# A streaming encoder step on one core: who issues a table copy, where six-row groups of gathers stand, and how a block opens

## What is computed

```
z = rmsnorm(x) @ w_in                       # 5888 columns: q,k,v of mixer A; q,k,v, gate of mixer B; two branch gates
oa = windowed attention with sinks (8 heads)
ob = retention with a state carried from block to block (4 heads)
y  = norm(ob) * silu(rg)
x1 = x + (sigmoid(ga) * (oa @ wa) + sigmoid(gb) * (y @ wb)) @ wo
h2 = rmsnorm(x1)
# expert retrieval: each row picks 128 of 16384 experts
a  = gelu(sum_d(h2 * u[idx]))               # "dots", 128 rows of u per token
x2 = x1 + sum_k(gate * a * v[idx])          # "values", 128 rows of v per token
out = rmsnorm(x2)
```

## Time and profile before

| | |
|---|---|
| median of 3 runs | 4240.19 us (4240.1 to 4246.9) |
| profiled execution: time, span | 4240.92 us, 4239.1 us |
| PE busy | 3299.9 us, 78% |
| DVE busy | 2488.8 us, 59% |
| POOL busy | 1872.0 us, 44% |
| ACT busy | 1047.1 us, 25% |
| granted PE clock, mean | 0.923 of full speed |
| DMA moved | 1554.55 MB, 367 GB/s |

### The profile page before, as it was taken

The page is one execution under the profiler, slowest core; times in us unless marked ns, Lnnn a source line. Parts: engine busy times, 40 slices in busy tenths (PEclk is TensorE's granted clock), DMA queues, the critical chain, the costliest instruction groups (busy, mean ns, idle before and its releaser), DMA issues.

```text
span 4239.1 us, 31704 instructions
## 1 busy us (share of the span) xinstructions
PE 3299.9 (78%) x8957; PEld 1646.9 (39%) x8957; DVE 2488.8 (59%) x5002; ACT 1047.1 (25%) x2851; POOL 1872.0 (44%) x1668
## 2 busy tenths in 40 slices
PE   8776599999657767638877977977977977777776
PEld 5453256666334444314333333333433432222222
DVE  0122078988846666436765765665665675675444
ACT  2111011111022122102333333333233333333332
POOL 1020147776725443203454454454454455455454
PEclk9877799999868878869999999999999999999999
DMA  9898989999978886527999999999999999999998
GB/s 354 298 297 296 317 268 413 411 413 404 385 310 309 331 321 244 193 115 302 421 421 420 406 421 406 421 419 409 407 422 411 415 421 419 415 415 422 422 420 351
DMA packets 302287, 1554.55 MB, mean 367 GB/s; under 512 B 31265, under 2 KB 58913, under 8 KB 179617
## 3 DMA queue, kind: packets, MB, share of 16 engines
q0 software_dynamic: 239616, 1342.28, 79.4%
q1 hardware_dynamic: 47920, 189.40, 11.4%
q10 hardware_dynamic: 14592, 21.10, 1.3%
HBM read 1509.02 MB, written 179.04 MB: 398 GB/s over the span
## 4 chain that ended last, share of the span: by engine, by line
DMA 27%; PE 17%; issue 6%; DVE 2%; ACT 1%; POOL 1%; POOLq 0%; ACTq 0%; DVEq 0%
DMA ring<-uv_d,IXD_p 27%; PE ps L1534 14%; PE ps L1504 3%; DVE ring L1735 1%; ACT dg L1584 1%; POOL ring L1853 1%; ACT GE_p L1578 0%; DVE DOT_p L1735 0%; DVE BV_p L945 0%; DVE ACC L1716 0%; ACTq L1583 0%; PE ps L1497 0%; PE ps L1519 0%; POOLq L1849 0%; DVE X L1726 0%
## 5 line engine op out<-in xcount | busy, mean ns | idle before, releaser
L1534 PE MATMUL ps<-ring,dg 128*128 128x512 f32 x3584 | 1698.9, 611 | 454.8 <-ACT dg L1584 433.7
L1853 POOL DMA_INDIRECT ring<-uv_d,IXD_p x896 | 1122.7, 1253 | 1330.4 <-PE ps L1534 1011.1
L1735 DVE CUSTOM_DVE_ANT_0 ring<-ring,H 128x1024 f32<-128x1024 f32 x896 | 1094.2, 1223 | 879.5 <-DMA ring<-uv_d,IXD_p 863.9
L1534 PEld LDWEIGHTS ps<-ring,dg 128*128 128x128 f32 x3584 | 651.4, 192 | 1381.6 <-ACT dg L1584 713.5
L1200 PE MATMUL ps<-w,xg 128*128 128x368 f32 x1792 | 554.3, 472 | 2.0 <-ACT SC_s L902 2.0
L1578 ACT ACTIVATE GE_p<-DOT_p 128x2 f32<-128x2 f32 x448 | 91.1, 203 | 1477.5 <-DVE DOT_p L1735 1477.5
L1200 PEld LDWEIGHTS ps<-w,xg 128*128 128x128 f32 x1792 | 340.4, 190 | 215.5 <-ACT SC_s L902 2.2
L1584 ACT ACTIVATE dg<-gdi,GE_p 128x128 f32<-128x128 f32 x896 | 310.6, 393 | 51.4 <-PE ps L1534 6.1
L1572 ACT ACTIVATE gdi<-ident,GD_p 128x128 f32<-128x128 f32 x896 | 303.0, 386 | 14.6 <-issue 14.5
L145 POOL DMA_DIRECT2D uv_d<-in_peer_u x128 | 68.3, 534 | 491.5 <-DMA uv_d<-in_peer_v 258.9
L1504 PE MATMUL ps<-wq,hT_p 128*128 128x512 f32 x448 | 224.3, 605 | 39.6 <-ACT hT_p L1542 39.6
(11 more groups left out here) (370 smaller groups left out, 2941.3 us busy)
## 6 DMA issues: line engine op xcount, KB each, us to landing
uv_d<-in_peer_u POOLq DMA_DIRECT2D x128, 512.0 KB, 6.4
uv_d<-in_peer_v POOLq DMA_DIRECT2D x128, 512.0 KB, 7.8
w<-in_w_in SPq DMA_DIRECT2D x8, 2944.0 KB, 14.9
w<-in_w_in SPq DMA_DIRECT2D x16, 1472.0 KB, 9.4
z_d<-zo ACTq DMA_DIRECT2D x16, 1288.0 KB, 18.6
ring<-uv_d,IXD_p POOLq DMA_INDIRECT x896, 11.1
gates_p<-z_d SPq DMA_DIRECT2D x7, 1536.0 KB, 10.0
wq_s<-in_peer_w_q SPq DMA_DIRECT2D x8, 1024.0 KB, 13.4
```

What stands on the lines that cost most here:

```text
L1534: mm = T.matmul(bank(6 + n), dg[:, k % DR, :], ring[:, k % RS, D + n * 512:D + (n + 1) * 512], start=(k == 0), stop=(k == NK - 1))
L1735: V.tensor_tensor_reduce(out=row, in0=row, in1=H2[:], scale=1.0, scalar=0.0, op0=ALU.mult, op1=ALU.add, accum_out=DOT[:, k:k + 1]).then_in ...
L1853: g.indirect_dma_start(ring[:, n % RS, :], None, uv_d, bass.IndirectOffsetOnAxis(ap=IXD[:, n:n + 1], axis=0)).then_inc(s_ring[n % RS], 16)
```

## The change

There are four edits.

1. The last 46 parts of the table are issued by SyncE (`rest_of_table`, a semaphore of its own, s_uvs) and no longer by GpSimd. In blocks 3 to 7 it issues three parts behind the load of the keys part, two behind the gates' load, and three at the end, behind the load of x; in block 8 two and four. GpSimd's stream in the stage is then gathers alone. The last stage waits for s_uvs too.
2. A point is cut into half points: value group (even) and dot group (odd). Three stand behind the softmax, three behind the copy of line 700, and two behind the retention norm. Dot group 1 thus stands behind the merge, and value group 2 between dot groups 1 and 2.
3. A block opens with the copies of q and k from PSUM, then the gate product; the v copy, the decayed k and the gate biases of the block before come after it.
4. Semaphore increments that nobody waits for are dropped (es, sm_neg, rok, mixa, keep).

```diff
+        s_uvs = sem("uv_table_rest")
+
+        def rest_of_table(sp, lo, hi):
+
+            for part in range(lo, min(hi, NEXP // P)):
+                sp.dma_start(uv_d[part * P:(part + 1) * P, 0:D], rows(t["peer_u"], part)).then_inc(s_uvs, 16)
+                sp.dma_start(uv_d[part * P:(part + 1) * P, D:], rows(t["peer_v"], part)).then_inc(s_uvs, 16)
+
...
                 act.wait_ge(s["sm_d"], blk + 1)
-                S.activation(es[:], es[:], ACT.Exp).then_inc(s["es"], 1)
+                S.activation(es[:], es[:], ACT.Exp)
...
                 step.settle()
-                v.sem_inc(s["rok"], 1)
...
                 V.tensor_tensor(z(RG, D), z(RG, D), yn[:].rearrange("p h n -> p (h n)"), ALU.mult).then_inc(s["ysil"], 1)
+
+            def dve_biases(v, blk):
+                v.wait_ge(s["z2"], 16 * blk + 16)
                 V.tensor_tensor(z(GA, 2 * D), z(GA, 2 * D), bg[:], ALU.add).then_inc(s["ga"], 1)
...
         def dve_block(v, blk, half, merge):
             step = Steps(v, s_vstep, STEPS_E if blk == 1 else STEPS_B + (blk - 2) * DVE_B)
+            v.wait_ge(s["t1"], blk + 1)
+            V.tensor_copy(qbT[:].rearrange("p h n -> p (h n)"), bank(1))
+            if blk <= 2:
+                v.wait_ge(s_tab, 32 * blk)
+            V.tensor_tensor(qdT[:].rearrange("p h n -> p (h n)"), bank(1), into[:].rearrange("p h n -> p (h n)"), ALU.mult)
+            V.tensor_copy(kaT[:, 1], ps[:, 3, 0:P]).then_inc(s["qkv"], 1)
+            if merge:
+                dve_gate(v, blk - 1)
+            wait_mixers(v, blk, half)
+            step.did(V.tensor_copy(va[:, 1], z(VA, P, half)))
+            for h in range(HB):
+                q = V.tensor_scalar(kdec[:, h, :], z(KB + h * DK, DK, half), outd[:, h:h + 1], None, ALU.mult)
+            q.then_inc(s["kdec"], 1)
             if merge:
                 if blk == 3:
                     v.wait_ge(s_bw, 16 * 8)
-                dve_gate(v, blk - 1)
-            wait_mixers(v, blk, half)
-            if blk <= 2:
-                v.wait_ge(s_tab, 32 * blk)
-            for h in range(HB):
-                q = V.tensor_scalar(kdec[:, h, :], z(KB + h * DK, DK, half), outd[:, h:h + 1], None, ALU.mult)
-            q.then_inc(s["kdec"], 1)
-            step.did(V.tensor_copy(va[:, 1], z(VA, P, half)))
-            v.wait_ge(s["t1"], blk + 1)
-            V.tensor_tensor(qdT[:].rearrange("p h n -> p (h n)"), bank(1), into[:].rearrange("p h n -> p (h n)"), ALU.mult)
-            V.tensor_copy(qbT[:].rearrange("p h n -> p (h n)"), bank(1))
-            V.tensor_copy(kaT[:, 1], ps[:, 3, 0:P]).then_inc(s["qkv"], 1)
+                dve_biases(v, blk - 1)
...
             dve_probs(v, blk, 2 * P)
-            dve_point(v, blk, 0)
-            dve_point(v, blk, 1)
+            for half_point in range(3):
+                dve_point(v, blk, half_point)
             if merge:
                 dve_merge(v, blk - 1)
             v.wait_ge(s["pt"], blk + 1)
             V.tensor_copy(PT[:, 4:8].rearrange("p h c n -> p (h c n)"), bank(2, 2)).then_inc(s["ptc"], 1)
-            dve_point(v, blk, 2)
+            for half_point in range(3, 6):
+                dve_point(v, blk, half_point)
             v.wait_ge(s["oat"], blk + 1)
             V.tensor_copy(oaT[:].rearrange("p j n -> p (j n)"), bank(0)).then_inc(s["oatc"], 1)
             V.tensor_copy(kaT[:, 0], kaT[:, 1])
-            V.tensor_copy(va[:, 0], va[:, 1]).then_inc(s["keep"], 1)
+            V.tensor_copy(va[:, 0], va[:, 1])
             dve_retention_norm(v, blk, 2, step)
-            dve_point(v, blk, 3)
+            for half_point in range(6, 8):
+                dve_point(v, blk, half_point)
             if merge:
                 dve_residual(v, blk - 1)
...
             def dve_point(v, blk, j):
-                grp = PTS * (blk - 2) + j
-                if blk > 2:
+                grp = PTS * (blk - 2) + j // 2
+                if j % 2:
+                    dve_expert_dots(v, grp)
+                elif blk > 2:
                     dve_expert_values(v, grp - PTS)
-                dve_expert_dots(v, grp)
...
                             load_keys_part(sp, blk + 1)
+                        part = TABLE_S + 8 * (blk - 3)
+                        if 2 < blk < NB - 1:
+                            rest_of_table(sp, part, part + 3)
+                            part += 3
                         if blk > 2:
                             sp.wait_ge(s["mixt"], blk)
                             load_gates(sp, blk)
+                            rest_of_table(sp, part, part + 2)
                             sp.wait_ge(s["x1"], blk)
                             sp.dma_start(rows(x1_d, blk - 1), X[:]).then_inc(s["x1st"], 16)
                             sp.wait_ge(s["h2"], blk)
                             sp.dma_start(rows(h2_d, blk - 1), HO[:]).then_inc(s["h2st"], 16)
                             sp.wait_ge(s["x1st"], 16 * blk)
                             load_rows(sp, blk)
+                            rest_of_table(sp, part + 2, part + 5 if blk < NB - 1 else NEXP // P)
...
                             pool_dots(g, grp)
-                            if blk > 2:
-                                part = TABLE_S + 2 * (grp - PTS)
-                                pool_table(g, part, min(part + 2, NEXP // P))
...
                     for i in range(2):
-                        g.wait_ge(s_uv[i], 32 * (NEXP // P // 2))
+                        g.wait_ge(s_uv[i], 32 * (TABLE_S // 2))
                         g.sem_inc(d["pool"], 1)
+                    g.wait_ge(s_uvs, 32 * (NEXP // P - TABLE_S))
+                    g.sem_inc(d["pool"], 1)
```

More of the change, by code:

```diff
@@ L228, in _ @@
                             mm.then_inc(s_mm, 1)
-        names = ("z1 z1b zq z2 xld t1 qkv scores sm_s sm_m sm_mx sm_neg sm_d es exp den rden prob pt ptc oat "
-                 "oatc st atm ro rok kvp stn stats var rs rstd yn silu ysil yt ytc ga gates ya mixa "
-                 "mixb mix mixt mixtc wo x1 ssq2 ms2 sq2 r2 h2 x1st h2st keep kdec").split()
+        names = ("z1 z1b zq z2 xld t1 qkv scores sm_s sm_m sm_mx sm_d exp den rden prob pt ptc oat "
+                 "oatc st atm ro kvp stn stats var rs rstd yn silu ysil yt ytc ga gates ya "
+                 "mixb mix mixt mixtc wo x1 ssq2 ms2 sq2 r2 h2 x1st h2st kdec").split()
         s = {n: sem("b_" + n) for n in names}
@@ L384, in dve_softmax @@
                 v.wait_ge(s["sm_mx"], blk + 1)
-                V.tensor_scalar(ngm[:], mx[:], -1.0, None, ALU.mult).then_inc(s["sm_neg"], 1)
+                V.tensor_scalar(ngm[:], mx[:], -1.0, None, ALU.mult)
                 V.tensor_tensor(es[:], sinks, mx[:], ALU.subtract).then_inc(s["sm_d"], 1)
@@ L426, in dve_merge @@
                 v.wait_ge(s["ya"], blk + 1)
-                V.tensor_tensor(z(GA, D), z(GA, D), bank(4, 2), ALU.mult).then_inc(s["mixa"], 1)
+                V.tensor_tensor(z(GA, D), z(GA, D), bank(4, 2), ALU.mult)
                 V.tensor_tensor(z(GB, D), z(GB, D), bank(6, 2), ALU.mult).then_inc(s["mixb"], 1)
@@ L593, in _ @@
                     dve_gate(v, 0)
+                    dve_biases(v, 0)
                     for h in range(HB):
@@ L831, in _ @@
                     V.memset(va[:, 0], 0.0)
-                    V.memset(alibi_c[:], NEG).then_inc(s["keep"], 1)
+                    V.memset(alibi_c[:], NEG)
                     V.memset(st[:], 0.0).then_inc(s["stn"], 1)
@@ L836, in _ @@
                     dve_gate(v, 1)
+                    dve_biases(v, 1)
                     dve_merge(v, 1)
@@ L1442, in _ @@
                     dve_gate(v, NB - 1)
+                    dve_biases(v, NB - 1)
                     for grp in range(LAST, TAIL - 1):
```

## The result

The changed kernel takes **4215.71 us** (median of 4 runs, 4213.54 to 4219.38), the kernel before 4242.14 (4 runs, 4240.1 to 4246.9): ratio 0.9942, 95% interval 0.9927 to 0.9956. The profiled execution took 4217.13 us (span 4215.3), 23.8 less than that of before. So it is faster, inside the range of 4183 to 4228, but the gain is 24 to 26 us where 42 were forecast.

What follows compares the result with a forecast made beforehand. No engine is full in mixer blocks 2 to 8; DVE's waits for gathers and PE's opening waits bound them. Gains of 15.2 (opening), 21.5 (copies and half points) and 5.4 (block 8) sum to 42.1, giving 4199 us, range 4183 to 4228.

Steps and rivals of the forecast that it cites:

- The bound: Whole kernel: the DMA-full last stage stays at 2313 us, so only blocks 2 to 8 of the mixer can gain.
- The opening, 15.2 us: Block openings: q and k copies fit under the silu wait, removing PE's 2.54 us wait before the scores, six times.
- The copies: Blocks 3 to 7: six of eight table parts move to where GpSimd can't put them, filling an empty DMA stretch.
- just fit: Block's end: six parts with stores and loads end about 32 us behind the dots, next value gather asked at 33.
- The half points, 21.5 us with the copies: Blocks 3 to 7: waits for gathers fall from 13.1 to 8.8 us a block, 4.3 each, 21.5 in all.
- The walk of block 7: Block 7, points replayed in the new order from time 0: the dots end at 48.7 us instead of 52.9.
- I take 3.7 (the landing then is 6.3): Block 7, second dot group: assumed wait of 3.7 us, between 1.5 and 6.5, with gates and two parts sharing the engines.
- the 9.3 of my upper bound: Second dot group: the middle landing of value gathers, 9.3 us, taken to give a wait of 6.5 us.
- what I had added to values 1 for the end of the parts: Block 7, second value group: 1.0 us added for the end of the six parts, moving its end from 15.5 to 16.5.
- PE's floor of 44.5: Block 8: PE's 44.5 us, above DVE's 44.0, sets its stretch instead of 49.9, a gain of 5.4 us.
- The signs: Profile checks: PE's scores wait gone, gated-transposes wait unchanged, openings 77 us apart, waits placed, pause's DMA busy, last stage 2313 us.
- One load, waits only move: Rival, 15%: gathers and copies are one load, landings stay near 9.3 us, only the opening gains, 4226 us.

Runs made afterwards that it cites:

- e1: Kernel before with only the new opening (q and k copies ahead of the gate product, biases and decayed k behind it): 4220.90 us, ratio 0.9954.
- e2: Kernel before with only the table copies moved to SyncE in sets of 3, 2 and 3, whole points, old opening: 4221.67 us, ratio 0.9959.
- f2: Changed kernel without the two parts behind the gates' load; four parts in the tail, twelve issued by GpSimd in the last stage: 4220.73 us, ratio 0.9872.
- e4: Changed kernel with sets of table copies 4, 0 and 4 instead of 3, 2 and 3: 4210.71 us, ratio 0.9934.

## Why the prediction was right and wrong

**The bound.** Right: nothing outside blocks 3 to 8 moved by more than 1.4 us.

**The opening, 15.2 us.** Right to the number: 2.6 a block from end to T0, six times, 15.6, hidden under the silu. What I missed is that the waits behind an earlier opening are shorter too, by some 7 us in e1; why was not traced.

**The copies.** The mechanism was right in its main part: landings fell from 9.3 to 6.1, the pause's empty stretch filled, and six parts "just fit" (values 1 wait 4.45; with eight they wait 9). The rule of the Trainium skill that I set against it (*DMA: Bandwidth & Descriptors*, "Issuing engines are not separate DMA queues": another issuer saves only the time of issue) doesn't cover it: e2 gains 18 us by its median, and 22 by its six blocks. Here an engine's stream, filled in order, also decided when a transfer could start and what stood ahead of it. That the engines are shared is true all the same, and it is what I under-rated below.

**The half points, 21.5 us with the copies.** This is the term that failed: the wait of dots 2 was sized too small. The walk of block 7 holds up to dots 2: they were asked for 24.9 us behind T0 (walk: 25.6) and wait 7.45 instead of "I take 3.7 (the landing then is 6.3)". The third row was asked for at 1609.27 and used at 1619.46, 10.2 us later, beyond the 9.3 of my upper bound. That bound came from a middle landing over all gathers, which is no bound for gathers issued right behind 3.6 MB on the other queue. By the rate of the last stage, 412 GB/s, that load alone is an estimated 9 us, and by my own 3.5 us a part nearly 11. The walk's subtraction was off as well: with values 2 ended at 28.8 and two dot products in between, a third row in use at 38.5 is a wait of 7.3 and not of 6.5 (it was in use at 38.0). f2 takes out the two parts and leaves everything else: dots 2 wait 3.2 to 5.0, mostly 3.2 to 3.8, and a block is 75.7 us against the forecast 76.9 (of the 1.2 too many, 1.0 is what I had added to values 1 for the end of the parts, which didn't come). So 3.7 is what dots 2 wait in a kernel without the two parts. I had counted them in, and the term held nothing for them: they are the 3.7 us that it missed in block 7, 3.4 in the mean of five.

In sum, blocks 3 to 7 have T0 to end of 259.3 us instead of 264.6: 5.3 us of gain where I had 21.5. Block 8 went from 49.8 to 46.8, 3.0 where I had 5.4. PE's floor of 44.5 didn't decide there, dots 2 did. 15.6 + 5.3 + 3.0 = 23.9, and the six blocks are 24.0 shorter.

**Luck.** The number lies in the range, but little of it comes from where I had put it. e1 alone has six blocks of 476.8, so edits 1 and 2 together add 1.7 us to edit 3 (5 by the ratios, whose intervals overlap), where I had 26.9 for them. That the total still came out inside is due to a range of 45 us and to the 7 us that the opening gave beyond its term. Edit 4 was forecast at nothing, and no run has it alone.

**The signs.** Right: PE's wait before the scores, the same last stage, the waits' places, DMA in the pause. Wrong: 80 us between openings, not 77, and PE's wait before the gated transposes, which I had unchanged: 83.7 us over six openings, from 62.8. With the merge earlier in the block PE is done earlier (it waits 22.0 us for merged rows where it waited 54.7), and the same idle time stands in another place.

**The rivals.** "One load, waits only move" came close. The waits of blocks 3 to 7 did little but move (62.5 us, 65.4 before), the cause it named holds for dots 2, and its 4226 would have been nearer with the opening at what e1 measured. But its condition failed: landings fell to 6.1, and e2 gains 22 us. The result lies between it and the forecast.

**Open.** The gates' own part of dots 2's wait was not taken away, since PE needs them in that place.

## What to carry to other kernels

An edit that gains alone can lose beside another, as edit 2 (7.5 us alone) lost 12 beside edits 1 and 3: walk the stream of the waiting engine for both at once, and write beside each of its gathers what the other queues are carrying in that moment. Bound a landing by the bytes issued just ahead of it on all queues, and not by the middle of all landings of before. And put bulk copies where nobody waits: f2 keeps the rest of the change, moves 12 of 46 parts to a stage that takes them for nothing, and doubles the gain (0.9872 against 0.9936).

## What was not expected of the hardware

SyncE's issues take longer while much is outstanding on its own queue. DMA issues that take it 0.34 us (the store of h2 at 1557.67) take up to 2.00 when the sixth of a row of table parts is issued, in the same opening of the changed kernel:

```profile
1565.58 0.50 SPq L244 DMA_DIRECT2D uv_d<-in_peer_u  x1
...
1569.88 2.00 SPq L244 DMA_DIRECT2D uv_d<-in_peer_u  x1
1571.93 1.53 SPq L245 DMA_DIRECT2D uv_d<-in_peer_v  x1
```

Over blocks 3 to 8 and the tail, an issue with up to nine transfers of this queue still to land takes 0.3 to 1.0 us in the middle, and one with twelve 1.3 to 3.2. More than twelve were never outstanding when one was issued, so SyncE seems to stand until one lands; that reason is inferred, and no run tests it. In the tail one 512 KB load (`ru<-x_d`) takes 0.60 us to issue before, 2.75 behind the changed kernel's four parts, and 10.78 in e4, where more stand ahead of it. The tail was no longer for it. A copy on this queue took 12.8 us (u) and 14.1 (v) from issue to landing in the middle, for 512 KB.
